# A one-core encoder layer in split precision: half square, low products, low sums and the values' unit in another order

## The chip, the core and the metric

One NeuronCore of a Trainium2 chip runs the whole layer. The metric is the device time of one execution in microseconds; lower is better. The weights and activations are float32 in HBM.

## What is computed

One layer of a streaming encoder for two groups: 512 prompt frames with 16 meta tokens in front, and 32 frames of a running stream with 256 cached keys and values. Cut to what matters:

```
h = RMSNorm(x)                       # the mean of squares of each token
p = h @ w_in                         # columns: GLU a | GLU b | q | k | v | gate_conv | gate_attn
A = silu(LayerNorm(depthwise_conv31(GLU))) @ w_pw2
z = q @ k.T / 8                      # 16 heads x 64, strictly causal
a = exp(log_sigmoid(z) + reverse cumulative sum of log_sigmoid(-z))
B = a @ v
x = x + (sigmoid(gate_conv) * A + sigmoid(gate_attn) * B) @ w_out
x = x + relu(RMSNorm(x) @ w_up)**2 @ w_down
y = RMSNorm(x)                       # and new keys, values and conv rows as outputs
```

## The kernel before, in words

**Split precision.** Each float32 operand is split into a high part (rounded to fp32r) and a low part (the rest). A projection is three products for each of 8 chunks of the inner dimension: high x high, high weights x low input, low weights x high input. `passes` (L505) issues them for two halves of the 560 (or 544) token columns: six matmuls per chunk, 48 per *unit* of 128 output columns. ScalarE rounds the weights (`high`, L904; for the first two units in halves, `high_half`, L936). POOL makes the low parts: for the first three units as eight instructions each (`low_parts`, L474), later by a DMA that adds onto a negated copy (`low`, L469). Weights pass through a ring of slots; SP loads a slot when its last user is through.

**Start.** `X_ORDER` is tiles 0, 4, 1, 2, 3 of the input. TensorE transposes each tile (L538), with `keep_warm` matmuls behind each, and VectorE copies it (L1301, L1304; ScalarE the upper halves of tiles 2 and 3, L956). ScalarE sums the squares of each tile (L922), but only half of tile 3; the other half is VectorE's (L1295, scaled L1297). Then come ScalarE's logarithm (L924, L926) and exponential (L928), five diagonal matrices `diag` (three on ScalarE L931, two on VectorE L1311), and TensorE's broadcast of them (L550). The rows of the six parameter vectors are transposed behind tile 1 (L542) and copied by VectorE (L1307); tile 3 waits for this copy. `normalise` (L1315) makes for each chunk the scaled input `n` (L1321); ScalarE rounds it to `r_hi` (L950) and VectorE subtracts for `r_lo` (L1324).

**First turn.** The units of queries (into `dense[:, 0]`) and keys (`dense[:, 1]`) run chunk by chunk as `r_lo` comes. Behind chunk 2 `conv_rows` (L561) transposes the convolution's rows; ScalarE copies them (L964) after the last chunk. The values' unit follows, in `z[:, 0:2]`, then the scores.

**Turns 1 to 7** (two heads each). In program order on TensorE: queries' unit, keys' unit, `keys_back` (keys of the last turn transposed into the queries' banks), cached keys, `cumulate` of the last turn's second head (L621), values' unit in the keys' banks, `values`, scores, values transposed back (L664), GLU units, `cumulate` of the first head, gate unit, scores of the second head. `cumulate` waits for `splo_done`, which counts three low parts of the softplus (L1384) and the low sums (`sums_low`, L1415) of each head. VectorE ends a turn with `sums_low` of the second head and begins the next with `q_low` (L1425), followed by convolution taps (L1342), `k_both` (L1430), `kT` (L1432, L1433) and more taps. ScalarE copies the queries, keys, cached keys, then the tokens of `keys_back` out of the queries' banks (`keys_kept`, L1026 and L1040; `ktok_kept`), then makes the probabilities.

**After the turns** come the rest of the gates, the second half of the layer and the output, all as units on TensorE; the change touches none of it but the place of one `sums_low`.

Of the kernel before, what the change touches and what calls it, by code (L numbers as in the profile page):

```python
# [79 lines left out]
def build(nc, x_prompt, x_sample, cache_k, cache_v, cache_conv, meta, g_mix, w_in, w_dw, b_dw,  # L80
# [24 lines left out]
    with ExitStack() as ctx:  # L105
# [156 lines left out]
        sp_done, sphi_done, splo_done = sem("sp_done"), sem("sphi_done"), sem("splo_done")  # L262
        cum_done, prob_done, pv_done = sem("cum_done"), sem("prob_done"), sem("pv_done")
# [67 lines left out]
        def _(sync):  # L331
# [40 lines left out]
            for n in range(4):  # L372
                if n < RING_LOOP:
                    sync.wait_ge(lo_done[n], 16 * LOOP_USES)
                if n == RING_LOOP:
                    sync.wait_ge(splo_done, 4 * HEADS)
# [46 lines left out]
        def _(pool):  # L423
# [52 lines left out]
            for s in range(2):  # L476
                pool.wait_ge(hi_first, s + 1)
                low_parts(s, range(0, LOW_PARTS // 2))
            for s in range(2):
                pool.wait_ge(hi_done, s + 1)  # L480
                low_parts(s, range(LOW_PARTS // 2, LOW_PARTS))
# [18 lines left out]
        def _(pe):  # L500
# [3 lines left out]
            def passes(wslot, out, m_hi, m_lo, c0, half, k):  # L504

                for n, (w, m) in enumerate(((w_hi, m_hi), (w_hi, m_lo), (w_lo, m_hi))):
# [13 lines left out]
            def keep_warm(count):  # L520
                for _ in range(count):
                    nc.tensor.matmul(z[:, 3, 0:P], ones[:], ones[:], start=True, stop=True)
# [5 lines left out]
            for j, t in enumerate(X_ORDER):  # L528
# [4 lines left out]
                if t == 3:  # L533

                    pe.wait_ge(rows_kept, 1)
# [4 lines left out]
                if t == 1:  # L540
                    pe.wait_ge(rows_loaded, 16 * 6)
                    nc.tensor.transpose(z[:, 1, 0:6 * KC], vec_rows[:], ident[0:6 * KC, 0:6 * KC]).then_inc(rows_turned, 1)  # L542
                keep_warm(2)


            for t, done, count in ((0, diag_act, 1), (3, diag_done, 1), (1, diag_act, 2), (4, diag_done, 2), (2, diag_act, 3)):
# [68 lines left out]
            def cumulate(head):  # L615

                pe.wait_ge(splo_done, 4 * head + 4)
# [15 lines left out]
                own(own_own, LAST, N_LAST, LAST)  # L633
                summed(negones, (2, n2 - n3), n3 + DEC, S3)
# [44 lines left out]
            def turn(i, prev=None):  # L679
# [10 lines left out]
                if first:  # L690
# [974 lines left out]
```

## Time and profile before

| | |
|---|---|
| median of 3 runs | 967.83 us (967.36 to 967.85) |
| the profiled execution | 967.5 us |
| its span, first to last instruction | 965.8 us |
| TensorE busy | 954.4 us (99%) |
| VectorE, ScalarE, POOL busy | 537.0, 529.9, 257.9 us |

The profile shows one execution. A busy TensorE says that instructions followed each other without a gap, not that its array was at its peak. "Idle before" is the gap in front of an instruction, with the engine and line whose signal ended it. Instructions merged into one line show the first start and the time from there to the last end.

### The profile page before, as it was taken

How to read it: one execution, taken by the hardware profiler on the slowest of the kernel's cores; microseconds unless marked ns; L12 is line 12 of the kernel's file. 1: busy time of each engine (PE TensorE's matmuls, PEld its weight loads, DVE VectorE, ACT ScalarE, POOL GpSimd, SP SyncE). 2: the span in 40 equal slices, each digit the busy share in tenths (PEclk: the TensorE clock that was granted, in tenths of full speed). 3: DMA queues.
4: the chain of work that ended last, by engine and by line, in shares of the span. 5: the costliest groups of instructions: out<-in, count | busy, mean ns of one | idle time of the engine just before them, and what ended most of it. 6: DMA issues, size and time to landing. Idle time of an engine off the chain costs nothing.

```text
span 965.8 us, 19515 instructions
## 1 busy us (share of the span) xinstructions
PE 954.4 (99%) x7577; PEld 933.6 (97%) x7577; DVE 537.0 (56%) x904; ACT 529.9 (55%) x827; POOL 257.9 (27%) x188
## 2 busy tenths in 40 slices
PE   8999999999999999999999999999999999999997
PEld 7999999999999999999999999999999999999997
DVE  6579898989898989998563322222111122221133
ACT  6787787878786877776933344333111133331143
POOL 5311010101011010101243333445433244453240
PEclk9999999999999999999999999999999999999999
DMA  6666667574848384749232233323323233233202
GB/s 179 154 153 141 159 124 173 108 182 98 183 100 191 91 185 105 169 109 227 71 105 83 79 93 101 88 87 94 103 88 87 66 88 87 87 109 92 61 23 93
DMA packets 165727, 111.35 MB, mean 115 GB/s; under 512 B 4637, under 2 KB 157485, under 8 KB 165690
## 3 DMA queue, kind: packets, MB, share of 16 engines
q1 hardware_dynamic: 147290, 77.72, 27.7%
q0 software_dynamic: 7632, 27.79, 16.1%
q10 hardware_dynamic: 10768, 5.32, 2.0%
q8 instruction: 26, 0.43, 0.2%
q14 instruction: 11, 0.09, 0.0%
HBM read 75.97 MB, written 7.06 MB: 86 GB/s over the span
## 4 chain that ended last, share of the span: by engine, by line
PE 97%; DMA 1%; ACT 1%; DVE 0%; ACTq 0%; issue 0%; DVEq 0%
PE dense L508 82%; PE z L621 3%; PE dense L811 3%; PE z L584 2%; PE z L654 2%; PE dense L664 1%; PE z L578 1%; PE z L508 1%; DMA w_lo<-w_raw 1%; DMA vec_rows<-in_g_final_dram 1%; PE z L588 1%; PE z L803 0%; PE z L640 0%; PE z L659 0%; ACTq L913 0%; PE z L550 0%
## 5 line engine op out<-in xcount | busy, mean ns | idle before, releaser
L492 POOL TENSOR_TENSOR w_lo<-w_raw,w_hi 128x1024 fp32r<-128x1024 f32 x80 | 192.3, 2407 | 294.9 <-ACT w_hi L904 294.9
L508 PE MATMUL dense<-r_hi,w_hi 128*128 128x272 f32 (+1 forms) x1264 | 265.5, 291 | 1.8 <-DVE r_lo L1324 1.5
L508 PE MATMUL dense<-r_hi,w_lo 128*128 128x272 f32 (+1 forms) x1264 | 262.8, 289 | 0.0
L508 PE MATMUL dense<-r_lo,w_hi 128*128 128x272 f32 (+1 forms) x1264 | 262.3, 289 | 0.0
L904 ACT ACTIVATE w_hi<-w_raw 128x1024 fp32r<-128x1024 f32 x134 | 140.7, 1052 | 113.5 <-PE dense L508 102.7
L508 PEld LDWEIGHTS dense<-r_hi,w_hi 128*128 128x128 f32 x1264 | 198.6, 188 | 4.1 <-DVE kT L1433 1.8
L508 PEld LDWEIGHTS dense<-r_hi,w_lo 128*128 128x128 f32 x1264 | 199.4, 188 | 0.0
L508 PEld LDWEIGHTS dense<-r_lo,w_hi 128*128 128x128 f32 x1264 | 198.9, 188 | 0.0
L1342 DVE SCALAR_TENSOR_TENSOR acc<-conv_in,cw_cur,acc 128x574 f32<-128x574 f32 x232 | 173.7, 810 | 0.7
L469 POOL DMA_DIRECT2D w_lo<-w_raw x53 | 45.2, 852 | 375.6 <-ACT w_lo L906 375.6
L508 PE MATMUL dense<-s_hi,w_hi 128*128 128x272 f32 x640 | 132.2, 288 | 0.0
L508 PE MATMUL dense<-s_hi,w_lo 128*128 128x272 f32 x640 | 131.6, 288 | 0.0
L508 PE MATMUL dense<-s_lo,w_hi 128*128 128x272 f32 x640 | 131.4, 287 | 0.0
L1524 DVE TENSOR_TENSOR xT<-dense,xT 128x544 f32 (+1 forms) x36 | 26.1, 724 | 159.3 <-PE dense L508 159.3
L508 PEld LDWEIGHTS dense<-s_lo,w_hi 128*128 128x128 f32 x640 | 100.0, 188 | 0.0
L508 PEld LDWEIGHTS dense<-s_hi,w_hi 128*128 128x128 f32 x640 | 99.7, 188 | 0.1
L508 PEld LDWEIGHTS dense<-s_hi,w_lo 128*128 128x128 f32 x640 | 99.7, 189 | 0.0
L1188 ACT ACTIVATE n<-n 128x544 f32<-128x544 f32 x32 | 21.1, 659 | 118.7 <-DVE n L1552 118.7
L1552 DVE SCALAR_TENSOR_TENSOR n<-dense,rstd 128x544 f32<-128x544 f32 x32 | 23.2, 725 | 95.5 <-PE dense L508 90.5
L906 ACT ACTIVATE w_lo<-w_raw 128x1024 fp32r<-128x1024 f32 x53 | 55.6, 1049 | 0.0
L508 PE MATMUL dense<-u_hi,w_hi 128*128 128x272 f32 x192 | 39.8, 288 | 0.0
L508 PE MATMUL dense<-u_hi,w_lo 128*128 128x272 f32 x192 | 39.5, 288 | 0.0
(265 smaller groups left out, 1318.7 us busy)
## 6 DMA issues: line engine op xcount, KB each, us to landing
w_raw<-in_w_in_dram SPq DMA_DIRECT2D x54, 512.0 KB, 5.3
w_lo<-w_raw POOLq DMA_DIRECT2D x53, 512.0 KB, 4.8
w_raw<-in_w_up_dram SPq DMA_DIRECT2D x32, 512.0 KB, 4.0
w_raw<-in_w_down_dram SPq DMA_DIRECT2D x32, 512.0 KB, 3.4
w_raw<-in_w_pw_dram SPq DMA_DIRECT2D x8, 512.0 KB, 3.5
w_raw<-in_w_out_dram SPq DMA_DIRECT2D x8, 512.0 KB, 3.4
x_tok<-in_x_prompt_dram SPq DMA_DIRECT2D x4, 512.0 KB, 6.3
out_dram<-v_tok ACTq DMA_DIRECT2D x8, 256.0 KB, 4.9
```

The source lines that it names most:

```text
L469: pool.dma_start(w_lo[:, s].bitcast(F32), w_raw[:, s], accum_op=ALU.add).then_inc(lo_done[s], 16)
L492: pool.tensor_tensor(w_lo[:, n], w_raw[:, n], w_hi[:, n].bitcast(F32), ALU.subtract).then_inc(lo_post, 1)
L508: mm = nc.tensor.matmul(out[:, h, 0:half], w[:, wslot, k, :], m[:, k, c0 + h * half:c0 + (h + 1) * half], start=(k == 0 and n == 0), stop= ...
L584: mm = nc.tensor.matmul(z[:, bank, off:off + SEQ - q0], k_both[:, hh, j * P:(j + 1) * P], qp[:, hh, q0:SEQ], start=False, stop=False, skip ...
L621: mm = nc.tensor.matmul(z[:, dst[0], dst[1]:dst[1] + n], m[:], part_[src], start=False, stop=False, skip_group_check=True)
L811: mm = nc.tensor.matmul(part_out(n, p), w[:, n, k, :], m[:, k, cols], start=(k == 0 and j == 0), stop=(k == KC - 1 and j == 2))
L904: done = nc.scalar.activation(w_hi[:, s], w_raw[:, s], ACT.Copy)
L906: done = nc.scalar.activation(w_lo[:, s], w_raw[:, s], ACT.Copy, scale=-1.0)
L1188: nc.scalar.activation(n32[:, n % 2, 0:OUTTOK], n32[:, n % 2, 0:OUTTOK], ACT.Square).then_inc(u32_done, 1)
L1342: nc.vector.scalar_tensor_tensor(dst, src, w, dst, ALU.mult, ALU.add).then_inc(tap_done, 1)
L1524: nc.vector.tensor_tensor(cols2(x_cur, HALFO), psum2(slot, HALFO), cols2(x_cur, HALFO), ALU.add).then_inc(emptied[slot], 1)
L1552: nc.vector.scalar_tensor_tensor(cols2(n32[:, n % 2, 0:OUTTOK], HALFO), psum2(n % 2, HALFO), 0.0, cols2(rstd[:, 0:OUTTOK], HALFO), ALU.max ...
```

## The change

On the start: VectorE makes tile 3's half square in front of the copy of tile 2, the third of the full tiles, TensorE transposes the vectors' rows behind tile 2 into another bank, two groups of `keep_warm` go, and three of the five diagonals are VectorE's. In the first two units, each chunk's high products of both units come first, waiting for `r_hi` alone, then the low ones. POOL makes the low parts of units 0 and 1 alternately. `conv_rows` moves behind the first values' unit, into a queries' bank. In the later turns the values' unit goes into the queries' banks once the tokens are copied out of them, and `sums_low` of the second head moves to the next turn, behind `q_low`, with a semaphore of its own that `cumulate` waits for in front of its first product with the sums.

```diff
@@ SP
                 if n == RING_LOOP:
-                    sync.wait_ge(splo_done, 4 * HEADS)
+                    sync.wait_ge(sumslo_done, HEADS)
@@ POOL
-            for s in range(2):
-                pool.wait_ge(hi_first, s + 1)
-                low_parts(s, range(0, LOW_PARTS // 2))
-            for s in range(2):
-                pool.wait_ge(hi_done, s + 1)
-                low_parts(s, range(LOW_PARTS // 2, LOW_PARTS))
+            for rounded, parts in ((hi_first, range(0, LOW_PARTS // 2)), (hi_done, range(LOW_PARTS // 2, LOW_PARTS))):
+                for part_ in parts:
+                    for s in range(2):
+                        if part_ == parts[0]:
+                            pool.wait_ge(rounded, s + 1)
+                        low_parts(s, (part_,))
@@ TensorE, start
-                if t == 3:
-                    pe.wait_ge(rows_kept, 1)
...
-                if t == 1:
+                if t == 2:
                     pe.wait_ge(rows_loaded, 16 * 6)
-                    nc.tensor.transpose(z[:, 1, 0:6 * KC], vec_rows[:], ident[0:6 * KC, 0:6 * KC]).then_inc(rows_turned, 1)
-                keep_warm(2)
+                    nc.tensor.transpose(z[:, 3, 0:6 * KC], vec_rows[:], ident[0:6 * KC, 0:6 * KC]).then_inc(rows_turned, 1)
+                if t in (0, 4, 3):
+                    keep_warm(2)
+            pe.wait_ge(rows_kept, 1)
-            for t, done, count in ((0, diag_act, 1), (3, diag_done, 1), (1, diag_act, 2), (4, diag_done, 2), (2, diag_act, 3)):
+            for t, done, count in ((0, diag_act, 1), (3, diag_done, 1), (4, diag_done, 2), (1, diag_act, 2), (2, diag_done, 3)):
@@ TensorE, conv_rows and cumulate
-                pe.wait_ge(upper_kept, 1)
+                pe.wait_ge(q_kept, 1)
...
-                    mm = nc.tensor.transpose(z[:, 0, k * 61:(k + 1) * 61], cw_rows[:, k * P:(k + 1) * P], ident[0:61, 0:61])
+                    mm = nc.tensor.transpose(dense[:, 0, 0, k * 61:(k + 1) * 61], cw_rows[:, k * P:(k + 1) * P], ident[0:61, 0:61])
...
-                pe.wait_ge(splo_done, 4 * head + 4)
+                pe.wait_ge(splo_done, 3 * head + 3)
...
                 own(own_own, LAST, N_LAST, LAST)
+                pe.wait_ge(sumslo_done, head + 1)
                 summed(negones, (2, n2 - n3), n3 + DEC, S3)
@@ TensorE, turn
                     for k in range(KC):
+                        pe.wait_ge(nhi_done, k + 1)
+                        pe.wait_ge(hi_first if k < KC // 2 else hi_done, 2)
+                        passes(0, dense[:, 0], r_hi, r_lo, META, HALFO, k, (0,))
+                        passes(1, dense[:, 1], r_hi, r_lo, 0, HALF, k, (0,))
                         pe.wait_ge(r_ready, k + 1)
-                        if k % (KC // LOW_PARTS) == 0:
-                            pe.wait_ge(lo_first[0], k * LOW_PARTS // KC + 1)
-                        last_q = passes(0, dense[:, 0], r_hi, r_lo, META, HALFO, k)
+                        pe.wait_ge(lo_first[0], k + 1)
+                        last_q = passes(0, dense[:, 0], r_hi, r_lo, META, HALFO, k, (1, 2))
...
-                        last_k = passes(1, dense[:, 1], r_hi, r_lo, 0, HALF, k)
-                        if k == 2:
-                            conv_rows()
+                        pe.wait_ge(lo_first[1], k + 1)
+                        last_k = passes(1, dense[:, 1], r_hi, r_lo, 0, HALF, k, (1, 2))
...
-                    pe.wait_ge(cw_kept, 1)
                     unit(2, None, out=z[:, 0:2])
+                    conv_rows()
...
-                    pe.wait_ge(k_kept, i + 1)
-                    unit(2, 1)
+                    pe.wait_ge(ktok_kept, i)
+                    unit(2, 0)
@@ ScalarE
-            for t in range(3):
+            for t in range(2):
                 nc.scalar.activation(diag[:, t, :], ident[:], ACT.Copy, scale=rstd_tok[:, t:t + 1]).then_inc(diag_act, 1)
...
             for k in range(KC):
                 split_high(k, TOK, n32_done, k + 1, r_hi[:, k, :], nhi_done)
-                if k < 2:
-                    act.wait_ge(tile_done, X_TILES - 1 + k)
-                    nc.scalar.activation(x_half(2 + k, 1), turned_half(2 + k, 1), ACT.Copy).then_inc(upper_kept, 1)
+                if k in (1, 2):
+                    t = k + 1
+                    act.wait_ge(tile_done, X_ORDER.index(t) + 1)
+                    nc.scalar.activation(x_half(t, 1), turned_half(t, 1), ACT.Copy).then_inc(upper_kept, 1)
-                if k == 2:
+                if k == 3:
                     high_half(0, 1, hi_done)
-                if k == 3:
                     high_half(1, 1, hi_done)
...
                 high_ahead(4)
+                if first:
+                    act.wait_ge(cw_turned, 1)
+                    nc.scalar.activation(cw[:].rearrange("p k r -> p (k r)"), dense[:, 0, 0, 0:KC * 61], ACT.Copy).then_inc(cw_kept, 1)
@@ VectorE
-                if t == 3:
-                    dve.wait_ge(x_loaded[t], 16)
-                    nc.vector.scalar_tensor_tensor(r_lo[:, KC - 1, 0:D // 2], x_tok[:, t, D // 2:], 1.0, x_tok[:, t, D // 2:], ALU.mult, ALU.mult, accum_out=half_sum[:, 0:1]).then_inc(square_added, 1)
+                if t == 2:
+                    dve.wait_ge(x_loaded[3], 16)
+                    nc.vector.scalar_tensor_tensor(r_lo[:, KC - 1, 0:D // 2], x_tok[:, 3, D // 2:], 1.0, x_tok[:, 3, D // 2:], ALU.mult, ALU.mult, accum_out=half_sum[:, 0:1]).then_inc(square_added, 1)
...
+                if t == 3:
+                    dve.wait_ge(rows_turned, 1)
+                    nc.vector.tensor_copy(vecs[:], z[:, 3, 0:6 * KC]).then_inc(rows_kept, 1)
+                    dve.wait_ge(root_done, 1)
+                    for d in (3, 4, 2):
+                        m = P if d < 4 else META + DEC
+                        nc.vector.tensor_scalar(diag[0:m, d, 0:m], ident[0:m, 0:m], rstd_tok[0:m, X_SCALE[d]:X_SCALE[d] + 1], None, ALU.mult).then_inc(diag_done, 1)
...
-                keep_keys(T_V, z[:, 0:2] if first else dense[:, 1], vT, v_kept)
+                keep_keys(T_V, z[:, 0:2] if first else dense[:, 0], vT, v_kept)
...
                 mm.then_inc(q_kept, 1)
+                if not first:
+                    sums_low(2 * i - 1)
                 conv_before(2)
...
                     softplus_low(2 * i + 1, n, 1)
-                sums_low(2 * i + 1)
```

## Rows read from the trace of the kernel before

**Rows 1.** The page's parts 1 and 2: busy time of the engines; granted TensorE clock in tenths.

```profile
PE 954.4 (99%) x7577; PEld 933.6 (97%) x7577; DVE 537.0 (56%) x904; ACT 529.9 (55%) x827; POOL 257.9 (27%) x188
...
PEclk9999999999999999999999999999999999999999
```

**Rows 2.** Who TensorE waited for: total us, times, longest us.

```profile
PE dense L508 <- DVE r_lo L1324: 1.5, 1, 1.5
...
PE z L588 <- DVE vT L1420: 0.9, 1, 0.9
```

**Rows 3.** The same for TensorE's weight loads.

```profile
PEld dense L508 <- DVE kT L1433: 1.8, 7, 0.3
...
PEld dense L664 <- DVE q_low L1425: 1.4, 7, 0.2
```

**Rows 4.** The chain that ended the first 45 us: start, us, what.

```profile
4.05 5.20 DMA vec_rows<-in_g_final_dram
```

**Rows 5.** The timeline, 8.9 to 13 us: start, us, instruction, [idle before].

```profile
8.91 1.22 DVE L1301 COPY xT<-dense 128x1024 f32<-128x1024 f32 x1 [0.76 <-PE dense L538]
...
11.72 0.68 DVE L1295 SCALAR_TENSOR_TENSOR r_lo<-x_tok 128x512 fp32r<-128x512 f32 x1
...
12.63 0.29 ACT L926 ACTIVATE rstd_tok<-rstd_tok,half_sum 128x1 f32<-128x1 f32 x1 [1.43 <-DVE half_sum L1297]
```

**Rows 6.** DMA issues between 2.2 and 2.6 us: size, us to landing.

```profile
x_tok<-in_x_prompt_dram SPq DMA_DIRECT2D x1, 512.0 KB, 7.6
```

**Rows 7.** The timeline, 19 to 32 us.

```profile
19.77 0.61 ACT L936 ACTIVATE w_hi<-w_raw 128x512 fp32r<-128x512 f32 x1
...
20.47 4.89 POOL L474 TENSOR_TENSOR w_lo<-w_raw,w_hi 128x128 fp32r<-128x128 f32 x8 [1.82 <-ACT w_hi L936]
...
21.26 0.61 ACT L936 ACTIVATE w_hi<-w_raw 128x512 fp32r<-128x512 f32 x1
...
23.32 0.71 PE L561 MATMUL z<-ident,cw_rows 61*128 61x61 f32 x8
...
25.85 4.92 POOL L474 TENSOR_TENSOR w_lo<-w_raw,w_hi 128x128 fp32r<-128x128 f32 x8 [0.49 <-ACT w_hi L904]
...
27.27 1.93 DVE L1324 TENSOR_TENSOR r_lo<-n,r_hi 128x560 fp32r<-128x560 f32 x2
...
27.97 0.56 ACT L964 ACTIVATE cw<-z 128x488 f32<-128x488 f32 x1
...
31.81 0.37 PE L508 MATMUL z<-r_hi,w_hi 128*128 128x280 f32 x1
```

**Rows 8.** POOL's instructions that write w_lo, 26.8 to 27.2 us: ns min/median/max.

```profile
L474 POOL TENSOR_TENSOR w_lo<-w_raw,w_hi x2: 457/724/990, 25.9 to 26.8; 128x128 fp32r<-128x128 f32 x2
```

**Rows 9.** The timeline, 51 to 55 us.

```profile
51.75 1.03 DVE L1415 TENSOR_TENSOR w_hi<-w_raw,w_hi 64x848 fp32r<-64x848 f32 x1
...
54.32 0.39 PE L621 MATMUL z<-sp_hi,tri 128*128 128x512 f32 x1
```

**Rows 10.** The timeline, 56 to 57 us and 75 to 81 us.

```profile
56.06 0.53 PE L621 MATMUL z<-w_hi,negones 128*128 128x400 f32 x2
56.43 0.41 PE L508 MATMUL dense<-r_hi,w_hi 128*128 128x272 f32 x2
...
75.60 1.46 DVE L1425 SCALAR_TENSOR_TENSOR q_low<-dense,q_twice 64x544 fp32r<-64x544 f32 x2
...
76.71 0.42 PE L508 MATMUL dense<-r_hi,w_lo 128*128 128x280 f32 x2
...
77.11 0.77 PE L664 MATMUL dense<-ident,kT 128*128 128x128 f32 x5
...
79.40 0.28 ACT L1040 ACTIVATE glu_tok<-dense 92x128 f32<-92x128 f32 x1
...
79.81 0.53 PE L621 MATMUL z<-w_hi,negones 128*128 128x400 f32 x2
...
80.32 0.40 PE L508 MATMUL dense<-r_hi,w_hi 128*128 128x280 f32 x1
```

More of the change, by code:

```diff
@@ L262, in build @@
         sp_done, sphi_done, splo_done = sem("sp_done"), sem("sphi_done"), sem("splo_done")
+        sumslo_done = sem("sumslo_done")
         cum_done, prob_done, pv_done = sem("cum_done"), sem("prob_done"), sem("pv_done")
@@ L502, in claim, with passes @@
                 pe.wait_ge(emptied[slot], n)
-            def passes(wslot, out, m_hi, m_lo, c0, half, k):
-                for n, (w, m) in enumerate(((w_hi, m_hi), (w_hi, m_lo), (w_lo, m_hi))):
+            def passes(wslot, out, m_hi, m_lo, c0, half, k, which=(0, 1, 2)):
+                three = ((w_hi, m_hi), (w_hi, m_lo), (w_lo, m_hi))
+                for n in which:
+                    w, m = three[n]
                     for h in range(2):
@@ L521, in keep_warm @@
                 for _ in range(count):
-                    nc.tensor.matmul(z[:, 3, 0:P], ones[:], ones[:], start=True, stop=True)
+                    nc.tensor.matmul(z[:, 2, 0:P], ones[:], ones[:], start=True, stop=True)
             pe.wait_ge(consts, 2)
@@ L721, in turn @@
                     cumulate(2 * i - 1)
-                    pe.wait_ge(k_kept, i + 1)
-                    unit(2, 1)
+                    pe.wait_ge(ktok_kept, i)
+                    unit(2, 0)
                     values(prev)
                 scores(i, 0, first)
-                if not first:
-                    pe.wait_ge(ktok_kept, i)
                 pe.wait_ge(v_kept, i + 1)
+                if first:
+                    pe.wait_ge(cw_kept, 1)
                 turn_back(vT, 0).then_inc(tile_done, 1)
@@ L962, in _ @@
                     high(2, raw_loop[2], 16, None, negated=False)
-            act.wait_ge(cw_turned, 1)
-            nc.scalar.activation(cw[:].rearrange("p k r -> p (k r)"), z[:, 0, 0:KC * 61], ACT.Copy).then_inc(cw_kept, 1)
             def log_sigmoid_parts(src, dst, half, tile_n, s_abs, s_exp, s_ln, count):
@@ L1074, in turn @@
                 high_ahead(4)
+                if first:
+                    act.wait_ge(cw_turned, 1)
+                    nc.scalar.activation(cw[:].rearrange("p k r -> p (k r)"), dense[:, 0, 0, 0:KC * 61], ACT.Copy).then_inc(cw_kept, 1)
                 if not first:
@@ L1304, in _ @@
                     nc.vector.tensor_copy(x_half(t, 0), turned_half(t, 0)).then_inc(emptied[j % 2], 1)
-                if t == 1:
-                    dve.wait_ge(rows_turned, 1)
-                    nc.vector.tensor_copy(vecs[:], z[:, 1, 0:6 * KC]).then_inc(rows_kept, 1)
-            dve.wait_ge(root_done, 1)
-            for t in (3, 4):
-                n = P if t < 4 else META + DEC
-                nc.vector.tensor_scalar(diag[0:n, t, 0:n], ident[0:n, 0:n], rstd_tok[0:n, X_SCALE[t]:X_SCALE[t] + 1], None, ALU.mult).then_inc(diag_done, 1)
             def normalise():
@@ L1414, in sums_low @@
                     dve.wait_ge(sumshi_done, head + 1)
-                    nc.vector.tensor_tensor(sums_both[UPPER], sums, sums_both[LOWER].bitcast(F32), ALU.subtract).then_inc(splo_done, 1)
+                    nc.vector.tensor_tensor(sums_both[UPPER], sums, sums_both[LOWER].bitcast(F32), ALU.subtract).then_inc(sumslo_done, 1)
                 def keep_keys(t, src, dst, kept):
@@ L1478, in _ @@
                 turn(before + 1, before)
+            dve.wait_ge(sumshi_done, 2 * KC)
+            nc.vector.tensor_tensor(sums_both[UPPER], sums, sums_both[LOWER].bitcast(F32), ALU.subtract).then_inc(sumslo_done, 1)
             for taps in CONV[2:]:
```

2 lines of the change are left out of this document (removed).

## Prediction

> **What bounds the kernel now.** The page's first two parts come first: TensorE is busy for 99% of the span and its granted clock never leaves the top level, 2.4 GHz [rows 1]. Only time in which it waits, or work taken from it, can shorten the run, and this change takes away no product. So the next view is the list of what TensorE waited for. It is short: 1.5 us once for the first low part of the normalised input, 0.9 us once for the kept values of the first turn [rows 2]. Under the weight loads stand two waits that come back in each of the seven later turns: 1.8 us in all for `kT`, 1.4 us for `q_low` [rows 3]. These are upper bounds, since a load's gap holds its ordinary hand-over too. A wait at the start has a history that this list doesn't show, so the chain of the first 45 us comes next. It runs through the landing of the last vector of parameters at 9.25 [rows 4], its transpose, two more input tiles, VectorE's half square, and ScalarE's logarithm. There ScalarE had idled for 1.43 us [rows 5]. Everything up to the first projection hangs on that.
>
> **Part 1, the half square and the vectors.** Before, VectorE made the half square of tile 3 behind the copy of tile 2, at 11.72; from there to ScalarE's start at 12.63 are 0.91 us for it and its scaling [rows 5]. Now it comes ahead of that copy. It can start when tile 3 has landed (issued at 2.2, 7.6 us to landing: 9.8 [rows 6]) and VectorE has copied tile 1 (8.91 + 1.22 = 10.13 [rows 5]). So it is over at 10.15 + 0.91 = 11.06, before ScalarE asks (12.63 - 1.43 = 11.20 [rows 5]): the whole 1.43 goes. What was in front on TensorE, the vectors' transpose, moves behind tile 2's transposes and no longer holds them up; its copy, two of the three `diag` of VectorE, and the third, taken from ScalarE, fit between 11.8 and 12.6. The third `diag` is the last of five that TensorE reads, so it isn't on the path. I take **1.42 us** earlier for all that follows. Bounds: 1.43, and 0 if tile 3 landed 1.4 us later.
>
> **Part 2, conv rows.** The eight transposes (0.71 us [rows 7]) stood inside the first two units. Now they stand behind the values' unit, where TensorE waited 0.9 us for VectorE's copy of the values anyway [rows 2]. So TensorE gets to the values' unit another 0.71 us earlier and loses nothing behind it. ScalarE's copy of them (0.56 us [rows 7]) moves behind its rounding for unit 4, and so delays the scores' logs of the first turn by 0.56. The cover: VectorE's low sums for the first cumulation ended at 51.75 + 1.03 = 52.78, and TensorE came for them at 54.32 [rows 9], so 1.5 us are there. If that cover were gone, 0.56 would be the cost, once. The POOL DMA for unit 5 is pushed back as much; the unit starts at 56.43 [rows 10], far behind.
>
> **Part 3, high products first.** Both units' high products of a chunk wait for `r_hi` and no more for `r_lo`, which lets TensorE begin up to 1.5 us sooner [rows 2]. But VectorE sets the last chunk. Its last `r_lo` ended at 27.27 + 1.93 = 29.20 [rows 7], now at 27.78; eight low products at 0.128 (pairs start 0.25 apart [rows 10]) and the cache keys bring TensorE to the values' unit at 28.9 at best. At worst, with nothing won, it is there at 31.81 [rows 7] - 1.42 - 0.71 = 29.68. I cost this part by itself at nothing, because of the next one.
>
> **Part 4, POOL's low parts.** The values' unit also needs its eight low parts. Before, they ended at 25.85 + 4.92 = 30.77, hidden by 1 us [rows 7]. What releases POOL's second batch is ScalarE's rounding of the first unit's second half. It stood behind the third chunk's rounding and now stands behind the fourth's: one chunk later (21.26 - 19.77 = 1.49 [rows 7]) and 1.42 earlier. So the batch starts at 20.5 as before. From there it is 16 parts: 4.89 + 4.92 = 9.81 us [rows 7]. A part takes 0.46 us, and 0.99 where it meets VectorE's `r_lo` [rows 8]. Before, six met one; with VectorE 1.42 ahead, the third chunk's is over before POOL starts, so five do: 9.81 - 0.5 = 9.3, and the end is at 29.8. That is later than either time for TensorE above, and sets the start of the values' unit: **29.9 instead of 31.81, 1.9 us**. Bounds: 1.4 us gained (no part spared, 30.3) and 2.4 (two spared). The alternation gives each unit its part in time; that unit 0's last part now comes some 2 us later pushes the load of unit 3 back, to a landing of 32.4 even at 7.6 us [rows 6]. ScalarE, with the queries' and keys' copies ahead of it, gets there at about the same time.
>
> What the Trainium skill says here ("SBUF — State Buffer", "Who interferes with whom") is that the port pair shared by VectorE and GpSimd is an exclusive lock, held for an instruction's whole length. By that each `r_lo` would hold POOL for its own 0.96 us and not for the 0.5 of the rows; 16 x 0.46 + 5 x 0.96 = 12.2, and the unit would start at 32.7, an estimate from the page's rule. The trace agrees with a hold, but not with its full length. I go by the rows, and the direction is my first rival.
>
> **Part 5, low sums and the values' bank, per turn.** At each turn's head VectorE made the low sums (1.03 us, as at 51.75 [rows 9]) and then `q_low`, 75.60 to 77.06. TensorE's unit pairs start 0.25 apart, so after the pair at 76.71 it could have gone on at 76.97; it did at 77.11, on `q_low`: 0.14 lost [rows 10]. With the sums moved behind, `q_low` needs only ScalarE's rounding and is done about 0.9 sooner. The sums then end near 77.2, and TensorE wants them after the first eight products of the cumulation, at about 79.4. Then the values' unit waited for VectorE's key copy. Between the last pair of sums and the unit lie 0.51 us (79.81 to 80.32), but only 0.37 where nothing holds it (56.06 to 56.43) [rows 10]: 0.14 lost. In the queries' banks it waits instead for ScalarE's copy out of them, done at 79.40 + 0.28 = 79.68 [rows 10], 0.3 us before TensorE comes. Seven times 0.28 is **1.9 us**. Bounds: 0 (another wait takes the place) and 3.2, all of the loads' idle time [rows 3]. VectorE's following taps start as before, since the sums and `q_low` together are no longer.
>
> **Sum.** 1.9 + 1.9 = 3.8 us. The profiled execution took 967.5 us; 963.7 by its own time. It lies 0.33 under the median of the three runs, 967.83, so I forecast **964.0**. All work behind 440 us is the same, with TensorE full, and moves as a block.
>
> **Rival 1: POOL holds the values' unit.** The unit waits for its whole eight parts. For it: POOL's end is already later than TensorE's in my own sum, and parts between 0.46 and 0.99 stand in these rows, with a median of 0.72 in one stretch [rows 8]. At 0.72 each, 16 parts end at 20.5 + 11.5 = 32.0, and the start gains nothing; 1.9 are left: 966.0. Against it: the same mix ran at 0.61 twice [rows 7]. 11%.
>
> **Rival 2: the waits of the loop change their names.** The new wait for ScalarE's copy has only 0.3 us of room. If ScalarE's copies come later by 0.6 in a turn, or the hand-over after `q_low` was ordinary, the loop gives nothing, and the start's 1.9 are left: 966.0. Against it: ScalarE had waited for the keys' unit before and starts those copies on the same signal. 9%.
>
> **Rival 3, slower: the clock falls at the start.** The change drops the spacers of ordinary matmuls after tiles 1 and 2, so that from about 8 to 11.3 TensorE does transposes alone. If the granted clock fell to 1.2 GHz for it, each microsecond of full-rate work until it is back costs another. The gain of 3.8 is gone after 3.8 us of such work, and it is slower by over 0.2% from 5.7: broadcasts, warm-up and three chunks, up to about 18. At 6 us: 964.0 + 6 = 970.0. Against it: the clock is at the top in every slice, the first too, though transposes and waits alternate there [rows 1], and the six warm-up matmuls in front of the projections stay. 5%.
>
> What speaks for it is a rule of the Trainium skill ("TensorE: Matmul & The Clock Gate", "Part 4: PE-mode transpose"): transposes do not count as activity for the clock in the way matmuls do. No row here shows TensorE on transposes alone for so long, so it can't be weighed further.
>
> **That it does not do what it says** would mean that the vectors' landing, not the half square, still holds the chain: `rows_kept` is asked for once more, in front of the broadcasts. It is met at about 12.0, before the first `diag` at 12.1. Only 0.1 us separates them, but a later landing costs just its own excess. 2%, inside the range.
>
> **How the numbers follow.** Forecast 73%: 964.0, on its own 963.0 to 965.0. Rivals 1 and 2: 966.0. Rival 3: 970. The range 963.0 to 966.2 holds the forecast and most of the two middle cases. 0.2% is 1.9 us, about what a measurement of this kernel can tell from no change: the bound lies at 965.9, and the middle cases, some 22% with the last one, fall to either side of it. Faster: 0.73 + 0.09 = 0.82. Same: 0.13. Slower: 0.05.
>
> **What the new profile would show.** ScalarE without its 1.43 us gap at the logarithm; TensorE's broadcasts at about 12.2; first projections at about 16.1; low parts of unit 2 done at 29.8 and its first product at 29.9, with a short wait on POOL; conv rows behind it, with at most 0.2 us of wait left on the values; no weight load waiting on `kT` or `q_low`, and each turn 0.28 us shorter. The forecast is wrong if unit 2 starts after 31, if a wait on ScalarE's token copies appears in the turns, or if the clock's row shows anything but nines.

## The result, and the profile after

The changed kernel takes **962.86 us** (median of 4 runs, 962.6 to 963.1) against 967.84 us for the kernel before (4 runs, 967.36 to 968.16): ratio 0.9949, 95% interval 0.9937 to 0.9961. That is 5 us, 0.5%, faster. The forecast was 964.0 with a range of 963.0 to 966.2; the direction is right, but the time lies 0.14 us below the range. The profiled execution took 962.6 us with a span of 960.9, against 967.5 and 965.8.

The page of the changed kernel, parts 1 and 2, answers to [rows 1]:

```profile
PE 951.3 (99%) x7569; PEld 933.2 (97%) x7569; DVE 535.5 (56%) x905; ACT 529.4 (55%) x826; POOL 257.1 (27%) x188
...
PEclk9999999999999999999999999999999999999999
```

TensorE's busy time fell by 3.1 us (954.4 to 951.3), though the change takes away no product, only spacers (eight records). Of the 3.1 us, 0.7 lie ahead of the broadcasts, where the spacers stood (10.85 busy before, 10.13 now); 2.4 lie between the first and the last values' unit (399.52 before, 397.08 now). So half of what was gained had been counted as busy time; how, the turns show below. The list of what TensorE waited for answers to [rows 2]:

```profile
PE dense L510 <- DMA w_lo<-w_raw: 0.7, 1, 0.7
PE dense L510 <- ACT r_hi L954: 0.6, 1, 0.6
...
PE z L589 <- DVE vT L1425: 0.3, 1, 0.3
```

The 1.5 us for `r_lo` are now 0.6 us for `r_hi`, the 0.9 for the values are 0.3. The wait for a DMA was 0.3 us before and is 0.7: here something was given back. In the list of the weight loads the rows for `kT` and `q_low` [rows 3] are gone altogether.

**The start.** The timeline of the changed kernel, from the half square to the broadcasts, answers to [rows 5]:

```profile
9.07 1.23 DVE L1313 COPY xT<-dense 128x1024 f32<-128x1024 f32 x1 [0.76 <-PE dense L537]
...
10.21 0.68 DVE L1300 SCALAR_TENSOR_TENSOR r_lo<-x_tok 128x512 fp32r<-128x512 f32 x1
...
11.13 0.28 ACT L930 ACTIVATE rstd_tok<-rstd_tok,half_sum 128x1 f32<-128x1 f32 x1
...
12.23 1.37 PE L551 MATMUL z<-diag,ones 128*128 128x128 f32 x10 [0.28 <-ACT diag L935]
```

The square stands right behind tile 1's copy, and ScalarE's line has no idle time in front of it. Before, it had 1.43, and TensorE's broadcasts began at 13.65. Then the first units, to the values' unit, which answers to [rows 7]:

```profile
16.15 0.74 PE L510 MATMUL dense<-r_hi,w_hi 128*128 128x272 f32 x4 [0.56 <-ACT r_hi L954]
...
20.30 9.24 POOL L475 TENSOR_TENSOR w_lo<-w_raw,w_hi 128x128 fp32r<-128x128 f32 x16 [3.31 <-ACT w_hi L940]
...
20.39 0.97 DVE L1329 TENSOR_TENSOR r_lo<-n,r_hi 128x560 fp32r<-128x560 f32 x1
...
29.34 0.38 PE L678 MATMUL z<-ident,ck_tok 128*128 128x128 f32 x2
29.59 0.52 PE L510 MATMUL z<-r_hi,w_hi 128*128 128x280 f32 x2
```

POOL's 16 parts end at 20.30 + 9.24 = 29.54, and the unit starts at 29.59 instead of 31.81: 2.22 us sooner. Of these 13.65 - 12.23 = 1.42 lie ahead of the broadcasts. The stretch from broadcasts to unit went from 31.81 - 13.65 = 18.16 to 29.59 - 12.23 = 17.36: 0.80.

**The turns.** Here the kernel before, turn 1, in rows that [rows 10] left out, TensorE's matmuls (PE) and weight loads (PEld):

```profile
77.96 0.48 PE L621 MATMUL z<-sp_hi,tri 128*128 128x512 f32 x1
...
80.32 0.30 PEld L508 LDWEIGHTS dense<-r_hi,w_hi 128*128 128x128 f32 x2 [0.25 <-DVE kT L1433]
...
80.68 0.42 PE L508 MATMUL dense<-r_lo,w_hi 128*128 128x280 f32 x2
```

And the same places in the changed kernel:

```profile
72.48 1.46 DVE L1430 SCALAR_TENSOR_TENSOR q_low<-dense,q_twice 64x544 fp32r<-64x544 f32 x2 [0.21 <-ACT q_twice L1062]
73.97 1.03 DVE L1420 TENSOR_TENSOR w_hi<-w_raw,w_hi 64x848 fp32r<-64x848 f32 x1
...
74.49 0.42 PE L510 MATMUL dense<-r_hi,w_lo 128*128 128x280 f32 x2
74.75 0.71 PE L666 MATMUL dense<-ident,kT 128*128 128x128 f32 x5
...
75.54 0.48 PE L622 MATMUL z<-sp_hi,tri 128*128 128x512 f32 x1
...
77.38 0.54 PE L622 MATMUL z<-w_hi,negones 128*128 128x400 f32 x2
77.63 0.31 PEld L510 LDWEIGHTS dense<-r_hi,w_hi 128*128 128x128 f32 x2
77.75 0.42 PE L510 MATMUL dense<-r_hi,w_hi 128*128 128x280 f32 x2
78.01 0.42 PE L510 MATMUL dense<-r_lo,w_hi 128*128 128x280 f32 x2
```

Four distances, before and after. Last pair to transposes: 0.40, 0.26. Transposes to cumulation: 77.96 - 77.11 = 0.85, now 0.79. Last sums to the values' unit: 0.51, 0.37. First pair of that unit to the second: 80.68 - 80.32 = 0.36, now 0.26. The first and the third are the gaps of the forecast, 0.14 each. The other two are new, 0.06 and 0.10: **a restart**. The weight load shows what it is. Unhindered it starts 0.12 ahead of its matmul (77.63, 77.75) beside the matmul before; after a wait both start together (80.32, 80.32), and the next pair comes 0.1 later. Together 0.44 a turn; the units at 80.32 and 382.59 before are at 77.75 and 377.39 now, so six turns went from 302.27 to 299.64, 50.38 to 49.94 each: 0.44 as well. Seven turns are 3.08.

The matmuls' list of waits has no row for this time, because the matmuls count as busy in it: between those two units TensorE is busy for all 302.27 us before and for all 299.64 now. The weight loads' list does have it. Its 1.4 us for `q_low` and 1.8 for `kT` in seven turns [rows 3] are 0.20 and 0.26 a turn; the distances give 0.20 (0.14 and 0.06) and 0.24 (0.14 and 0.10). The forecast had that list and took its 3.2 us as an upper bound only.

That a load is drawn ahead of running matmuls is what the Trainium skill says too ("TensorE: Matmul & The Clock Gate", "Step-by-step: what each phase is for"); the trace agrees, with 0.12 us. It gives no price for losing the lead; the rows do.

**Given back.** The last turn's unit and the first gate unit behind the turns, the kernel before:

```profile
432.25 0.42 PE L508 MATMUL dense<-r_hi,w_hi 128*128 128x272 f32 x2
...
441.59 0.52 PE L508 MATMUL dense<-r_hi,w_hi 128*128 128x272 f32 x2 [0.35 <-DMA w_lo<-w_raw]
```

The changed kernel, with the chain of waits ahead of 442 us (start, us, what) in the second fence:

```profile
426.95 0.42 PE L510 MATMUL dense<-r_hi,w_hi 128*128 128x272 f32 x2
...
436.68 0.40 PE L510 MATMUL dense<-r_hi,w_hi 128*128 128x272 f32 x1 [0.73 <-DMA w_lo<-w_raw]
```

```profile
429.59 0.95 ACT w_lo L910
430.55 0.28 issue
430.83 5.80 DMA w_lo<-w_raw
436.63 0.04 issue
436.68 5.42 PE dense L510 x41
```

TensorE is 5.30 us ahead at the first row and 4.91 at the second: 9.34 us between them before, 9.73 now. The account of these two executions closes: 2.22 + 3.08 - 0.39 = 4.91, and the span is 4.9 shorter. The DMA was issued 3.88 after the unit in both (436.13 before, 430.83 now) and took 5.42 before, 5.80 now. The 0.39 is not a fixed price: the same distance is 9.43 to 9.53 in the traces of b_sums, b_bank, b_square and a_keys_banks, whose units come at 430.94 to 433.89, and 9.44 in a_pool_blocks, whose unit comes at 426.92 as here.

### The profile page after: what moved, and what is told of

Read it like the earlier page. It is cut to its first block, busy times and chain, and to the rows that moved or that the text cites. A ratio compares the mean times of both kernels' runs of the same rounds, so it can differ in the third digit from the quotient of the medians.

```text
span 960.9 us, 19501 instructions
## 1 busy us (share of the span) xinstructions
PE 951.3 (99%) x7569; PEld 933.2 (97%) x7569; DVE 535.5 (56%) x905; ACT 529.4 (55%) x826; POOL 257.1 (27%) x188
## 4 chain that ended last, share of the span: by engine, by line
PE 97%; ACT 1%; DMA 1%; DVE 0%; issue 0%; ACTq 0%; DVEq 0%
PE dense L510 82%; PE z L622 3%; PE dense L815 3%; PE z L585 2%; PE z L656 2%; PE z L579 1%; PE dense L666 1%; PE z L510 1%; DMA w_lo<-w_raw 1%; ACT n L926 1%; PE z L589 1%; DMA x_tok<-in_x_prompt_dram 0%; PE z L807 0%; PE z L642 0%; PE z L661 0%; PE z L551 0%
```

## Experiments

Kernels named a_ are the changed one with an edit, those named b_ the one before with an edit. Theory 1 and theory 2 in the quotes are the account drawn from the two traces and its rival, as each quote puts them. The kernel before was timed again beside each group of runs, so its median differs a little (967.56 to 968.01). "Period" is the distance of one turn to the next on TensorE, 50.38 before and 49.94 after.

### The turns: which of the two moves

**a_keys_banks**: the values' unit back into the keys' banks.

```diff
-                    pe.wait_ge(ktok_kept, i)
-                    unit(2, 0)
+                    pe.wait_ge(k_kept, i + 1)
+                    unit(2, 1)
```

> The changed kernel (962.86 us) with the values' unit of turns 1 to 7 back in the keys' banks, behind VectorE's key copy. Theory 1, a wait of TensorE costs its gap and a slow restart of 0.10 us besides, and the low sums in front of the key copy have made that copy later against TensorE: in the changed kernel's turn 1 the copy ends at 78.21 and the unit starts at 77.75, so 0.5 + 0.1 a turn, 4.2 in all: 967.0 us. Theory 2, only the gap counts and it is the 0.14 of before: 1.0 in all, 963.9 us.

967.1 us against 967.7, 0.9995 (0.9985 to 1.0004): all that the turns gave is gone, and most of what the start gave. Its waits of the weight loads, and the timeline of turn 2:

```profile
PEld dense L510 <- DVE kT L1442: 4.4, 7, 0.6
```

```profile
128.33 0.53 PE L622 MATMUL z<-w_hi,negones 128*128 128x400 f32 x2
129.22 0.53 PE L510 MATMUL dense<-r_hi,w_hi 128*128 128x280 f32 x2 [0.35 <-DVE kT L1442]
129.58 0.43 PE L510 MATMUL dense<-r_lo,w_hi 128*128 128x280 f32 x2
```

The distance is 0.89 where the changed kernel has 0.37, and the restart of 0.10 (0.36 to the next pair) comes on top: 0.62 a turn, which with 49.94 makes the period's 50.56. The loads' list says the same: 4.4 us in seven turns, 0.63 each.

**a_wait_keys**: the queries' banks kept, and the wait for the key copy added.

```diff
                     pe.wait_ge(ktok_kept, i)
+                    pe.wait_ge(k_kept, i + 1)
                     unit(2, 0)
```

> The changed kernel, values' unit in the queries' banks as there, but with the wait for VectorE's key copy in front of it as well. It parts the wait from the bank. If the wait is all that the bank spares: the same as the run with the unit in the keys' banks, 967.0 us by theory 1. If the bank itself matters (who reads which bank while TensorE writes): nearer to 962.9 us.

968.03 against 967.7, 1.0001 (0.9992 to 1.0011), period 50.54 to 50.58. So it is the wait and not the bank. Against a_keys_banks 0.9 us more are lost. In the two profiled executions its start was 0.35 later, and another 0.6 went between the first values' unit and the next. The traces show where. ScalarE's last two issues of the value tokens took 1.45 and 1.10 us in a_wait_keys, 0.70 and 0.64 in a_keys_banks; ScalarE's next rounding (`sp_hi`) began at 48.90 instead of 47.33, VectorE's first tap at 58.97 instead of 58.06, and the key copy ended at 79.48 instead of 78.59, with TensorE waiting for it. The same long issues stand in the traces of a_out_late (1.48, 1.10) and a_round_first (1.53, 1.17), where nothing waits for the key copy and that stretch is as long as in the changed kernel (48.19 and 48.16, there 48.16). Why the issues take longer in some executions no run shows, nor whether the two medians differ for this reason.

**a_sums_back**: the low sums back at the end of the turn, in front of `q_low`.

```diff
                     softplus_low(2 * i + 1, n, 1)
+                sums_low(2 * i + 1)
...
                 mm.then_inc(q_kept, 1)
-                if not first:
-                    sums_low(2 * i - 1)
```

> The changed kernel with the low sums of the second head back at the end of the turn, in front of q_low. Theory 1 (gap and restart): 0.14 of gap and 0.06 of restart at the transposes come back in each of seven turns, 1.4 us: 964.3 us. Theory 2 (gap alone): 1.0 us, 963.9 us. If the two parts of the turns don't depend on each other in this direction, the values' unit starts without a wait as in the changed kernel.

964.01 against 967.7, 0.9963 (0.9948 to 0.9977). The times of the two theories are too close to tell apart by it; the timeline does, in turn 2:

```profile
126.45 0.53 PEld L666 LDWEIGHTS dense<-ident,kT 128*128 128x128 f32 x5 [0.20 <-DVE q_low L1430]
```

The last pair is at 126.06, the transposes at 126.45 (0.39, not 0.26), the cumulation at 127.30 (0.85, not 0.79): 0.20 a turn, and the period is 50.14. The profiled execution is the slowest of the five (965.25): its broadcasts began at 13.01, and its first turn lost 0.7 more to `q_low` behind the same long issues of ScalarE (1.53 and 1.15).

**b_turns**: the kernel before with both moves, the bank as in b_bank and the sums as in b_sums.

> The kernel before (967.84 us) with both parts of the turns and nothing of the start: low sums behind q_low, values' unit in the queries' banks. Theory 1: 0.44 us a turn, 3.1 in all, of which the DMA of the low weights after the turns may take back up to 0.4: 964.8 to 965.1 us. Theory 2: 0.28 a turn, 1.9 in all: 965.9 us.

964.71 against 967.7, 0.9971 (0.9960 to 0.9982), period 49.94. The turns alone bring 3.0 us, not the 1.9 of the forecast.

**b_bank**: the kernel before with the values' unit in the queries' banks alone.

```diff
-                    pe.wait_ge(k_kept, i + 1)
-                    unit(2, 1)
+                    pe.wait_ge(ktok_kept, i)
+                    unit(2, 0)
```

> The kernel before with the values' unit in the queries' banks and nothing else. Theory 1 (gap 0.14 and restart 0.10 in each of seven turns): 1.7 us won, 966.0 us. Theory 2 (gap alone): 1.0 us, 966.7 us.

966.35 against 968.01, 0.9983 (0.9974 to 0.9992): 1.7 us for seven waits of 0.14 and restarts of 0.10, which is 0.24 a turn (period 50.13).

**b_sums**: the kernel before with the sums moved alone.

```diff
                     softplus_low(2 * i + 1, n, 1)
-                sums_low(2 * i + 1)
...
                 mm.then_inc(q_kept, 1)
+                if not first:
+                    sums_low(2 * i - 1)
```

> The kernel before (967.7 us) with the low sums moved behind q_low and nothing else. Theory 1, the two parts of the turns depend on each other: 0.2 us a turn is won at q_low, but the key copy comes 0.2 later and TensorE is there 0.2 earlier, so the values' unit in the keys' banks waits 0.5 instead of 0.14: 0.17 lost a turn, 1.2 in all, 968.9 us. Theory 2, each part pays by itself: 1.4 us won, 966.3 us.

969.35 against 968.01, 1.0014 (1.0004 to 1.0023): **slower**. VectorE and TensorE in turn 2:

```profile
125.78 1.46 DVE L1427 SCALAR_TENSOR_TENSOR q_low<-dense,q_twice 64x544 fp32r<-64x544 f32 x2 [0.21 <-ACT q_twice L1062]
127.27 1.04 DVE L1417 TENSOR_TENSOR w_hi<-w_raw,w_hi 64x848 fp32r<-64x848 f32 x1
...
130.67 0.53 PE L622 MATMUL z<-w_hi,negones 128*128 128x400 f32 x2
131.57 0.53 PE L509 MATMUL dense<-r_hi,w_hi 128*128 128x280 f32 x2 [0.36 <-DVE kT L1437]
```

```profile
PEld dense L509 <- DVE kT L1437: 4.4, 7, 0.6
```

With the sums in front, VectorE had work while ScalarE rounded the queries. Without them it idles 0.21, and its row up to the key copy ends later as seen from a TensorE that no longer waits for `q_low`. What the one wait gives, the other takes, and more: the loads' list, in the second fence, has 4.4 us for `kT` where it had 1.8 and 1.4 [rows 3], so 1.2 more. Only together with the other bank does the move pay: the two gains don't add up from their single trials (1.7 and -1.3 against 3.0).

### The start

**b_square**: the kernel before with the half square alone in its new place.

```diff
-                if t == 3:
-                    dve.wait_ge(x_loaded[t], 16)
+                if t == 2:
+                    dve.wait_ge(x_loaded[3], 16)
```

> The kernel before with the half square made ahead of tile 2's copy and nothing else. The chain theory: the first broadcasts need VectorE's diagonal of tile 3, which stands behind the copy of tile 3 (12.51 to 13.2), and that waits for the vectors' landing at 9.25 through two tiles; ScalarE's 1.43 us go, but no more than 0.2 is won: 967.5 us. If the half square alone was what held the start: 1.4 us won, 966.3 us.

967.39 against 968.01, 0.9993 (0.9984 to 1.0002): 0.6 us, near the first expectation, and the interval reaches to no change. VectorE's and TensorE's timeline:

```profile
12.89 0.69 DVE L1304 COPY xT<-dense 128x512 f32<-128x512 f32 x1 [0.61 <-PE z L538]
...
13.50 0.43 DVE L1311 TENSOR_SCALAR diag<-ident,rstd_tok 128x128 f32<-128x128 f32 x2
...
13.83 1.38 PE L550 MATMUL z<-diag,ones 128*128 128x112 f32 x9 [0.31 <-DVE diag L1311]
```

ScalarE's gap is gone, but tile 3's copy, still behind the vectors' transpose and its own, now stands in front of VectorE's diagonals, and TensorE waits for these. So by this trace the 1.42 needs the diagonals' and the transpose's new places too; neither was tried by itself.

**a_square_late**: the changed kernel with the square back behind tile 2's copy.

```diff
-                if t == 2:
+                if t == 3:
                     dve.wait_ge(x_loaded[3], 16)
```

> The changed kernel (962.86 us) with the half square back behind the copy of tile 2. The chain theory: it is ready 0.75 us later (copy 0.7 ahead of it), ScalarE's exponential and all behind it follow: 963.6 us. If POOL's low parts hold the values' unit in any case: they are chained to the same exponential through the rounding, so the same; if DMA landings hold it: 962.9 us.

963.16 against 967.78, 0.9952 (0.9937 to 0.9968). By time it can't be told from the changed kernel. In the trace ScalarE idles again, and TensorE's wait for the first `diag` is 0.9 instead of 0.3:

```profile
11.44 0.29 ACT L930 ACTIVATE rstd_tok<-rstd_tok,half_sum 128x1 f32<-128x1 f32 x1 [0.37 <-DVE half_sum L1302]
```

It is half of what was expected: with the vectors' rows out of its way VectorE gets to the square sooner in either order, so the order alone is worth 0.37.

**a_one_by_one**: each unit's high and low products together again.

```diff
-                        passes(0, dense[:, 0], r_hi, r_lo, META, HALFO, k, (0,))
-                        passes(1, dense[:, 1], r_hi, r_lo, 0, HALF, k, (0,))
                         pe.wait_ge(r_ready, k + 1)
```

> The changed kernel with each chunk's six products of a unit in one piece again, after r_lo. TensorE starts at about 16.9 instead of 16.15 and must follow VectorE: the last chunk's r_lo isn't late then, so its queue ends at about 29.9 instead of 29.6. Theory 1, TensorE sets the values' unit: 0.3 us lost, 963.2 us. Theory 2, POOL sets it (its last part ends at 29.54 in the changed kernel): up to 0.1 lost, 962.9 us.

962.89 against 967.78, 0.9950 (0.9937 to 0.9964): no difference by time. In the trace its broadcasts begin at 12.29 and the values' unit at 30.22, 17.93 us later and not 17.36. TensorE's and POOL's part of it:

```profile
16.97 0.49 PE L510 MATMUL dense<-r_hi,w_hi 128*128 128x272 f32 x2 [1.33 <-DVE r_lo L1327]
...
20.34 9.24 POOL L475 TENSOR_TENSOR w_lo<-w_raw,w_hi 128x128 fp32r<-128x128 f32 x16 [3.31 <-ACT w_hi L938]
```

POOL is done at 29.58 here too, the unit starts 0.64 later. So in this variant TensorE sets the start, and in the changed kernel both arrive within 0.1 us. Part 3 is worth about 0.6 on that stretch, not nothing; the medians don't show it, since the starts of single executions differ by more (last section).

**a_conv_rows_early**: the eight transposes back inside the first units, into their old bank.

```diff
                         last_k = passes(1, dense[:, 1], r_hi, r_lo, 0, HALF, k, (1, 2))
+                        if k == 2:
+                            conv_rows()
...
                     unit(2, None, out=z[:, 0:2])
-                    conv_rows()
```

> The changed kernel with the conv rows' eight transposes back behind chunk 2 and their copy behind the last chunk. They take 0.71 us there; part of it falls into waits for VectorE that TensorE has in chunks 3 to 6 now (some 0.4 us by the trace), and the 0.7 us behind the values' unit go back to being a wait for the values. Net 0.2 to 0.6 lost: 963.1 to 963.5 us. If the place doesn't matter: 962.9 us.

962.71 against 967.78, 0.9946 (0.9933 to 0.9960): no difference. That is less than the 0.2 to 0.6 expected. From broadcasts to unit it is 12.40 to 29.86, 17.46, only 0.1 more than 17.36, and even that lies behind the first units: the cached keys, just ahead of the unit, begin 17.12 after the broadcasts here and 17.11 in the changed kernel (29.34 - 12.23). In the first units TensorE has slack that hides the transposes; the three gaps of 0.2 that its weight loads have there for `r_lo` are gone. Behind the values' unit they are hidden as well, for here the wait for the values is 0.9 again instead of 0.3.

**a_pool_blocks**: POOL makes four parts of unit 0, then four of unit 1, as before.

```diff
-                for part_ in parts:
-                    for s in range(2):
...
+            for s in range(2):
+                pool.wait_ge(hi_first, s + 1)
+                low_parts(s, range(0, LOW_PARTS // 2))
...
```

> The changed kernel with POOL's low parts unit by unit again. Unit 1's fifth part is then done at about 23.2 instead of 21.3; TensorE asks for it at about 23.8 in the changed kernel. Expected: no wait, 962.9 us, since the last part of all comes at the same time. If the alternation is needed for the high-first order: a wait at chunk 4, 0.3 us or more lost.

963.23 against 967.78, 0.9952 (0.9939 to 0.9966): no difference that can be told. Broadcasts to unit 17.61 (11.94 to 29.55), 0.25 more; POOL 9.24 as ever. The 0.25 lies ahead of POOL's batch, which begins at 20.27, 8.33 after the broadcasts and not 8.07.

### What is given back

**a_round_first**: ScalarE rounds the weights of the gate unit ahead of the last head's probabilities.

```diff
-            probabilities(2 * KC - 1, 1)
+            act.wait_ge(cum_done, 2 * KC)
             high_post(0, 1, True)
+            probabilities(2 * KC - 1, 1)
```

> The changed kernel (962.86 us) with ScalarE's rounding of the weights in ring slot 3 ahead of the last head's probabilities, behind the same wait for the cumulation. In the changed kernel TensorE waits 0.7 us for the DMA of these low weights after the turns. The rounding, 2.1 us, begins 1.4 us earlier, so the DMA is issued 1.4 earlier; the probabilities come 2.1 later and have 4 us of room. All of the 0.7 should go, 962.2 us; 962.9 us if the wait is for the DMA queue and not for its issue.

962.88 against 968.01, 0.9946 (0.9932 to 0.9959): nothing gained. The DMA goes out at 430.12, and its share of the issues (size, us to landing) reads:

```profile
w_lo<-w_raw POOLq DMA_DIRECT2D x1, 512.0 KB, 6.9
```

From the last turn's unit (427.62) it is issued 2.50 later, in the changed kernel 3.88; it lands 9.45 later, there 9.68. Issued 1.4 us sooner, it takes 1.1 us longer. In that stretch the DMA engines are full, as the windows view of the changed kernel shows (last two numbers: DMA share, where 1 and more is full, and GB/s); the second fence is a_out_late, below, where less is moved:

```profile
426.00:434.00 8.00, 8.00 (x63) 7.28 (x63) 8.00 (x12) 6.82 (x10) 0.85 (x1) 1.00 1.18 286
```

```profile
426.00:434.00 8.00, 8.00 (x62) 7.72 (x62) 8.00 (x12) 6.82 (x11) 0.85 (x1) 1.00 1.03 259
```

**a_out_late**: the last keys' tokens, 0.25 MB, go out behind the rounding for slot 3.

```diff
-            keys_out(KC - 1)
...
             high_post(0, 3, True)
+            keys_out(KC - 1)
```

> The changed kernel (962.9 us) with the last turn's key tokens sent out after three more weight roundings. In the changed kernel the low weights' DMA after the turns takes 5.8 us (5.4 before) with the DMA engines full, and TensorE waits 0.7 us for it. If the 0.25 MB sent out beside it is what slows it: the DMA lands 0.5 to 0.8 us sooner, 962.2 us. If it is the next weights' loads of SP: no change, 962.9 us.

961.83 against 967.56, 0.9942 (0.9928 to 0.9956). The DMA now takes 4.6 us instead of 5.8:

```profile
w_lo<-w_raw POOLq DMA_DIRECT2D x1, 512.0 KB, 4.6
```

```profile
427.64 0.42 PE L510 MATMUL dense<-r_hi,w_hi 128*128 128x272 f32 x2
...
436.56 0.52 PE L510 MATMUL dense<-r_hi,w_hi 128*128 128x272 f32 x2
```

There is no wait in front of the gate unit any more: 8.92 us between the two rows, where it was 9.73, and 9.34 in the kernel before. So what delayed the low parts was a transfer beside them, not their issue.

**a_round_out_late**: the edit of a_round_first and that of a_out_late together.

> Both: slot 3 rounded ahead of the probabilities and the key tokens sent out later. Rounding first alone issued the DMA 1.1 us sooner and it landed no sooner. If the tokens sent out were what filled the engines: the wait of 0.7 us goes whole, 962.2 us; if SP's loads do: 962.9 us.

**961.75 us** (961.74 to 962.1) against 967.56, 0.9941 (0.9927 to 0.9954), again 8.92 between the two places. It has the lowest median of all. Against the kernel before it is 5.8 us faster, the changed kernel 5.0, so it is ahead by about 0.8; the two were not timed side by side and their intervals overlap, but the distance in the trace, 8.92 for 9.73, says the same. The earlier rounding adds nothing that can be measured: the DMA is issued 1.4 us sooner than in a_out_late, takes 6.0 us for 4.6, and lands 8.5 us after the last turn's unit in both.

## Where the forecast was right, and why it was too small

**Part 1, half square and vectors: right.** 1.42 us forecast, 1.42 measured, broadcasts at 12.23 (forecast 12.2). That both digits agree is luck: in four traces with the old start the broadcasts begin at 13.55 to 14.18, in ten with the new one at 11.92 to 13.01. The means, 13.86 and 12.48, are 1.37 apart. It needed its companions: alone the square brought 0.6, not clear of no change (b_square), and put back alone it cost 0.4 by the trace (a_square_late).

**Part 2, conv rows: right in the sum, wrong in the reason.** The sentence "TensorE gets to the values' unit another 0.71 us earlier" does not hold where slack between chunks covers them; a_conv_rows_early found the cached keys no later (17.12 and 17.11) and the unit 0.1 later. Behind the unit they are hidden, as put, but 0.28 of wait is left and not at most 0.2.

**Part 3, high products first: "at nothing" was too little.** Without it the start is 0.6 later (a_one_by_one). The best case of its bounds, 28.9 for TensorE, did not come: it was ready at about 29.5 (the cached keys at 29.34, and 0.13 from there to the unit in a_one_by_one, 30.09 to 30.22). So it was no more than 0.1 ahead of POOL, where the forecast had 0.1 to 0.9.

**Part 4, POOL: nearly right.** Batch from 20.30, 9.24 us, end 29.54; forecast 20.5, 9.3 and 29.8. Unit start 29.59 instead of 29.9. The start gave 2.22 us for 1.9.

**Part 5, the turns: the step that failed.** "Seven times 0.28 is 1.9 us" priced each wait at the gap in front of the instruction. A wait also costs the restart behind it, 0.06 at the transposes and 0.10 at the unit. Measured: 0.44 a turn, 3.08 us, inside the bounds of 0 and 3.2 given for the part. The upper one came from the loads' idle time, which holds what the matmuls' rows don't show; to take the lower reading as the likely one was the mistake. The forecast's ground for it, that "a load's gap holds its ordinary hand-over too", doesn't hold: with the waits gone no gap is listed there. Nor did the range carry the part's bound: its own 3.2 would have led to 962.7, and the range stopped at 963.0. That both waits go, and the copy out of the queries' banks is in time, was right. "VectorE's following taps start as before" was off by 0.2: it now idles for the queries' rounding. In the keys' banks that would have cost 0.62 a turn (a_keys_banks, b_sums); the new bank hides it.

**The sum: "moves as a block" failed too**, the other way. TensorE, 5.30 us ahead, met low weights that were only 4.9 us ahead, and waited 0.7 instead of 0.3; the transfer had been issued 5.30 ahead and took 0.38 longer. How much of this comes of being earlier is open, as the distance of 9.34 is 9.43 to 9.53 in kernels that come at most 1.3 us earlier, or even later. With the right sizes the sum is 2.22 + 3.08 - 0.39 = 4.91 where 3.8 was forecast; the 1.1 us between them are 0.3 at the start, 1.2 in the turns, and 0.4 given back. The first and the last nearly cancel, which is luck; with the 3.08 alone put right the forecast would have been 962.8.

**Rivals.** Rival 1, POOL holding the unit until 32: no, nor the 32.7 by the rule of the Trainium skill ("SBUF — State Buffer", "Who interferes with whom"), which has the shared port held for a whole instruction. In the changed kernel's batch a part takes 0.46, and five that meet an `r_lo` take 0.85 to 0.96; each meeting cost POOL 0.4 to 0.5 us, about half an `r_lo`. The rule fits in kind and not in size. Rival 2, new names for the same waits: not in the changed kernel, but b_sums is just that, slower by 1.3. Rival 3, the clock: nines throughout. Between one spacer's end (8.16) and the next one's start (11.34) TensorE did nothing but transposes, 25 records and 2.82 us busy, and the granted clock of these 3.2 us was 1.00, the top level, 2.4 GHz. The view shows 2 us of them; the clock is the third number from the end:

```profile
9.30:11.30 2.00, 1.65 (x15) 1.39 (x14) 1.97 (x5) 1.88 (x6) 0.00 (x0) 1.00 1.20 298
```

The rule that transposes don't count as activity for the clock ("TensorE: Matmul & The Clock Gate", "Part 4: PE-mode transpose", again the Trainium skill) changed nothing over these 3.2 us; longer stretches no run here shows.

**Still open**: why ScalarE's issues of the value tokens take 1.3 us in some executions and 2.7 in others, and how much of the 0.4 given back comes of TensorE being earlier.

## What to carry to other kernels

On a dense TensorE, price a wait by the distance of starts from the last instruction before it to the second one behind it, and compare with the same place unstalled. The gap between the matmuls held only a part, here 0.28 of 0.44, and the matmuls' list of waits nothing; the weight loads' list had it all, within 0.02 us a wait. Price a move between engines as a set: b_sums alone lost 1.3 us and together with the other bank it gained as much. And when TensorE comes out of a loop earlier, look at the first transfer it meets: if the DMA engines are full, issuing that transfer sooner brings nothing, while moving an unurgent one out of its way does.

## What the runs showed of the hardware

- A weight load that has waited loses its lead of 0.12 us over its matmul, and the pair behind comes 0.36 after the first instead of 0.26.
- A 512 KB accumulating DMA took 5.8 us in the changed kernel, 4.6 with 0.25 MB less beside it, and 6.9 when issued 1.4 us sooner. Without a change to either it took 5.4 to 5.8 from trace to trace.
- POOL's part and VectorE's `r_lo` slow each other: 0.46 to 0.96 and 0.74 to 1.01. Once, at 16.0 us in the changed kernel, the part took 1.00 and the `r_lo` stayed at 0.74. The batch of 16 took 9.24 us in the changed kernel and in two variants of its start.
- The broadcasts of identical start code began between 11.92 and 13.01 in ten traces, while the stretch from there to the values' unit was 17.33 to 17.36 in the seven of them with the same first units. So the start's parts were compared over that stretch, and not by the clock time of the unit; and differences of 0.3 us there don't show in the medians.
